# A router between the halves of a projection: logits, ranks and tables of a mixture-of-experts kernel in another order

## The reference

```
x = x + mixer(h) ... @ w_o                       # [1024,1024] @ [1024,1024]
h = rmsnorm(x, norm2_w)
g_prob = softmax(h @ rg_w + rg_b)                # 8 groups
g_sel = the best group, p_group its probability
e_logits = (h @ re_w + re_b)[of the group g_sel] # 8 experts of that group
top_p, top_i = top_k(softmax(e_logits), 2)
gate = p_group * top_p / sum(top_p)
expert = g_sel * 8 + top_i                       # 2 of 64 experts for each token
# every pair (token, expert) is put in its expert's list; then for each expert
hb = silu(xb @ w_gate[e]) * (xb @ w_up[e]);  y[tokens] += gate * (hb @ w_down[e])
x = rmsnorm(x + y, final_norm_w)
```

## Time and profile before

| | |
|---|---|
| median of 3 runs | 2660.02 us (2655.1 to 2666.81) |
| profiled execution | 2654.39 us |
| its span, first to last instruction | 2652.6 us |
| TensorE busy | 2371.0 us, 89% |
| VectorE / ScalarE / GpSimd busy | 765.9 / 551.8 / 574.0 us |
| moved by DMA | 537.41 MB, mean 203 GB/s |
| mean granted TensorE clock | 0.940 |

### The profile page before, as it was taken

How to read it: one execution, slowest core, us unless ns; L and a number is a source line. 1 busy time by engine, 2 the same in 40 slices (tenths; PEclk the granted TensorE clock), 3 DMA queues, 4 the chain that set the end, 5 groups by cost and what they waited for, 6 DMA issues and landing times.

```text
span 2652.6 us, 42516 instructions
## 1 busy us (share of the span) xinstructions
PE 2371.0 (89%) x18656; PEld 1537.5 (58%) x18656; DVE 765.9 (29%) x1615; ACT 551.8 (21%) x1147; POOL 574.0 (22%) x409
## 2 busy tenths in 40 slices
PE   7999988788699999999999997999999988888882
PEld 6887776677576654788887455433334434444440
DVE  4111325555345524223223352211111111111114
ACT  4111223332455412211111221101001111011012
POOL 5333433332111113423322001111111111111110
PEclk9999999998799999999999997999999899999996
DMA  4223110101110022211113306999999999999997
GB/s 188 87 98 126 70 65 27 35 11 73 65 64 1 1 88 72 80 47 49 50 55 126 145 24 263 428 429 430 429 429 429 429 430 428 427 427 429 427 412 209
DMA packets 69777, 537.41 MB, mean 203 GB/s; under 512 B 13464, under 2 KB 13720, under 8 KB 43600
## 3 DMA queue, kind: packets, MB, share of 16 engines
q1 hardware_dynamic: 54688, 501.79, 46.0%
q10 hardware_dynamic: 4656, 15.99, 2.0%
q0 software_dynamic: 10240, 16.82, 1.7%
HBM read 503.08 MB, written 43.52 MB: 206 GB/s over the span
## 4 chain that ended last, share of the span: by engine, by line
PE 71%; DMA 17%; DVE 5%; ACT 4%; issue 3%; ACTq 0%; POOL 0%; POOLq 0%; DVEq 0%; SPq 0%
PE banks L219 47%; DMA arena<-in_wg 15%; PE banks L224 8%; PE banks L226 8%; PE banks L225 7%; DMA arena<-yb 1%; ACT arena L229 1%; ACT arena L1594 1%; PE banks L2800 1%; DVE arena L1573 0%; DVE arena L2776 0%; DVE arena L1121 0%; DVE arena L1141 0%; DMA arena<-in_x 0%; DVE arena L828 0%
## 5 line engine op out<-in xcount | busy, mean ns | idle before, releaser
L219 PE MATMUL banks<-arena 64*64 64x64 f32 (+14 forms) x15424 | 1697.8, 350 | 200.8 <-DMA arena<-in_wg 62.2
L219 PEld LDWEIGHTS banks<-arena 64*64 64x64 f32 (+5 forms) x15424 | 980.0, 157 | 859.9 <-issue 706.0
L229 ACT ACTIVATE arena<-banks 128x512 f32<-128x512 f32 (+6 forms) x381 | 219.8, 587 | 1434.3 <-PE banks L219 624.2
L2794 POOL DMA_INDIRECT yb<-arena x64 | 64.7, 1012 | 810.2 <-DVE arena L2905 810.2
L2905 DVE TENSOR_SCALAR arena<-banks,arena 128x512 f32<-128x512 f32 x64 | 48.1, 751 | 524.3 <-PE banks L219 524.3
L224 PE MATMUL banks<-h1h,w2s 128*128 128x512 f32 x448 | 176.8, 395 | 1.7 <-DVE h1l L1959 1.7
L225 PE MATMUL banks<-h1l,w2s 128*128 128x512 f32 x448 | 174.9, 390 | 0.0
L226 PE MATMUL banks<-h1h,w2s 128*128 128x512 f32 x448 | 174.7, 390 | 0.0
L224 PE MATMUL banks<-hh,wlo 128*128 128x512 f32 x432 | 172.5, 399 | 0.0
L226 PE MATMUL banks<-hh,wlo 128*128 128x512 f32 x432 | 171.1, 396 | 0.0
L225 PE MATMUL banks<-hl,wlo 128*128 128x512 f32 x432 | 169.8, 393 | 0.0
(11 more groups left out here) (240 smaller groups left out, 1522.8 us busy)
## 6 DMA issues: line engine op xcount, KB each, us to landing
arena<-in_wg SPq DMA_DIRECT2D x64, 2048.0 KB, 31.5
arena<-in_wu SPq DMA_DIRECT2D x64, 2048.0 KB, 24.5
arena<-in_wd SPq DMA_DIRECT2D x64, 2048.0 KB, 32.7
arena<-in_w SPq DMA_DIRECT2D x55, 512.0 KB, 3.2
spill<-arena SPq DMA_DIRECT2D x27, 512.0 KB, 2.6
arena<-spill SPq DMA_DIRECT2D x27, 512.0 KB, 5.9
arena<-in_wo SPq DMA_DIRECT2D x16, 512.0 KB, 7.3
arena<-in_x SPq DMA_DIRECT2D x12, 512.0 KB, 5.3
```

The lines of the kernel that those rows point to most:

```text
L219: return pe.e.matmul(o, l, r, start=start, stop=stop)
L229: return act.e.activation(o, i, ACT.Copy)
L2794: return pool.e.indirect_dma_start(yb, bass.IndirectOffsetOnAxis(ap=six[:, col:col + 1].bitcast(U32), axis=0), src[:, :], None, bounds_che ...
```

## The change

TensorE now does the logits of block j-1 between the two projection halves of block j, then the second half, then `pe_count(j - 1)` and `pe_table(j - 2)`. At the end come logits 7, table 6, count 7 and table 7. In `pe_count` the matmuls over older blocks come ahead of the wait for `expert_hot`, then the triangular one that completes the ranks, and the running total last. VectorE runs the route of block j-1 between its two residual adds of block j, norms block j, and makes the table of block j-1 behind that. GpSimd zeroes the three `xg` buffers in `pool_table`, ahead of the last two one-hot rows, instead of one by one ahead of the gathers.

```diff
--- before.py
+++ after.py
@@ -2482,14 +2482,16 @@
                     pe.wait_ge(s(f"wo{c}"), 32)
                     t = mm(pe, u.t[:, :], yT[:, c, j * 128:(j + 1) * 128], wo2[:, c, n * 512:(n + 1) * 512], c == 0, c == 7)
                 t.then_inc(u.full.sem, 1)
+
+                if n == 0 and j:
+                    pe_logits(pe, j - 1)
             if j:
-                pe_logits(pe, j - 1)
-            if j >= 3:
-                pe_table(pe, j - 3)
+                pe_count(pe, j - 1)
+            if j >= 2:
+                pe_table(pe, j - 2)
         pe_logits(pe, 7)
-        pe_table(pe, 5)
+        pe_table(pe, 6)
         pe_count(pe, 7)
-        pe_table(pe, 6)
         pe_table(pe, 7)
         for key in ("count", "tables"):
             ps.release(key)
@@ -2510,21 +2512,19 @@
         for c in range(8):
             t = mm(pe, u.t[:, 0:72], h2T[j % 2][:, c, :], rw[:, c, :], c == 0, c == 7)
         t.then_inc(u.full.sem, 1)
-        if j:
-            pe_count(pe, j - 1)
 
     def pe_count(pe, j):
 
         uc = ps["count"]
         pe.wait_ge(s("con2"), 16)
+        u = ps.open(pe, ("rank", j))
+        for i in range(j):
+            mm(pe, u.t[:, 0:64], C("ones"), Ah[:, i, :], i == 0, False)
         pe.wait_ge(s("expert_hot"), j + 1)
+        mm(pe, u.t[:, 0:64], K2("tri"), Ah[:, j, :], j == 0, True).then_inc(u.full.sem, 1)
         tc = mm(pe, uc.t[:, 0:64], C("ones"), Ah[:, j, :], j == 0, j == 7)
         if j == 7:
             tc.then_inc(uc.full.sem, 1)
-        u = ps.open(pe, ("rank", j))
-        for i in range(j):
-            mm(pe, u.t[:, 0:64], C("ones"), Ah[:, i, :], i == 0, False)
-        mm(pe, u.t[:, 0:64], K2("tri"), Ah[:, j, :], j == 0, True).then_inc(u.full.sem, 1)
 
 
 
@@ -2540,11 +2540,21 @@
     def pool_table(pool):
         pool.wait_ge(s("con2"), 16)
         for n in range(16):
+            if n == 14:
+                pool_zero_xg(pool)
             pool.wait_ge(s("rank_found"), n // 2 + 1)
             if n >= 4:
                 pool.wait_ge(s("table_step"), n - 3)
             pool.e.tensor_scalar(ohm[n % 4][:, :], K2("im"), rk_[:, n % 2, n // 2:n // 2 + 1], None,
                                  ALU.is_equal).then_inc(s("rows").sem, 1)
+
+    def pool_zero_xg(pool):
+
+        pool.wait_ge(s("h2"), 8)
+        u = ps["logits", 7]
+        pool.wait_ge(u.full, u.v)
+        for i in range(3):
+            pool.e.memset(xg[i][:, :], 0.0).then_inc(s("xg_zero").sem, 1)
 
     def dve_table(dve, j):
         e = dve.e
@@ -2620,10 +2630,8 @@
                 u = ps["out2", j, n]
                 dve.wait_ge(u.full, u.v)
                 dve.e.tensor_tensor(xres[:, j, ns], xres[:, j, ns], u.t[:, :], ALU.add).then_inc(u.free.sem, 1)
-            if j:
-                dve_route(dve, j - 1)
-            if j >= 2:
-                dve_table(dve, j - 2)
+                if n == 0 and j:
+                    dve_route(dve, j - 1)
             dve.wait_ge(s("res2_sq"), j + 1)
             dve.e.tensor_scalar(m, m, 1.0 / D, 1e-6, ALU.mult, ALU.add).then_inc(s("res2_mean").sem, 1)
             dve.wait_ge(s("res2_root"), j + 1)
@@ -2636,8 +2644,9 @@
 
             dve.e.scalar_tensor_tensor(h2[j % 3].rearrange("p (c n) -> p n c", c=8), xres[:, j, :].rearrange("p (n c) -> p n c", c=8),
                                        m, n2b.rearrange("p (n c) -> p n c", c=8), ALU.mult, ALU.mult).then_inc(s("h2").sem, 1)
+            if j:
+                dve_table(dve, j - 1)
         dve_route(dve, 7)
-        dve_table(dve, 6)
         dve_table(dve, 7)
         dve_table_out(dve)
 
@@ -2943,7 +2952,6 @@
         for j in range(5, 8):
             pool.wait_ge(*h2_stored(j))
         for i in range(3):
-            pool.e.memset(xg[i][:, :], 0.0).then_inc(s("xg_zero").sem, 1)
             pool.wait_ge(s("xg_zero"), i + 1)
             pool_fetch(pool, i)
         for e in range(NEXP):
```

## The result

| | before | changed |
|---|---|---|
| median of 20 runs each | 2658.14 us | 2667.11 us |
| ratio, 95% interval | | 1.0029 (1.0022 to 1.0037) |
| profiled execution, and its span | 2654.39, 2652.6 | 2666.17, 2664.4 us |
| router's start | 1457.56 | 1460.81 us |
| start to A (last projection half full) | 141.15 | 157.84 us |

The changed kernel is slower by 0.29%, 9.0 us by the medians and 7.7 us by the ratio. That lies inside the whole range (2658 to 2677 us) and inside that of the forecast case alone (+3 to +13 us). The changed kernel's router began 3.25 us later in its profiled execution.

The account below looks back on a forecast made before the run. The experts' weight stream was taken to set the pace, so the end moves with G: A 16.8 us later, A to G 6.9 us shorter, sum +9.9 us, 2664.3 us profiled, 2669.9 us carried to the median; range 2658 to 2677 us.

Parts of the forecast that it names:

- forecast case: Whole kernel: the main case, +9.9 us with its own range of +3 to +13; chance 0.60.
- What bounds the kernel: Expert stage: the weight stream at 429 GB/s sets the pace, so the end moves as G moves.
- G: The moment when the gate projection of expert 0 is full; before, 42.2 us after A.
- The stall in block 1: Router, block 1: TensorE waits at logits 0 for h2 of block 0, 6.4 us.
- Its clock: Behind the block 1 stall: TensorE's granted clock falls to 0.50, costing 4.3 us (bounds 0 and 6.0).
- A itself: Last projection half full: 16.8 us later, from 6.1 us of work moved ahead of it and 10.7 of stall and clock.
- A to G: Router tail to first gate projection: 35.3 us in place of 42.2, 6.9 us better (5.5 to 10.2).
- The gather under the stream: First gather, now lying under weight chunks 3 to 7: 6.5 us, where it took 3.22 before.
- The store of h2 7: Tail, block 7: issued at A + 5.85, lands at A + 18.7, 3 us before it is needed.
- wait in every block: Rival, middle blocks: h2 comes later than TensorE reaches the logits; +16 us at 1 us a block; chance 0.15.
- The clock did fall: Against the rival that the clock does not fall behind the block 1 stall, +5 us; chance 0.12.
- the stream did run dry: Against the rival that the weight stream never runs dry and the end follows A alone, +4 us; chance 0.10.

Follow-up runs that it names:

- Late gain waits: Changed kernel with VectorE's waits for norm gain, router bias and constants moved to their first use; ratio to before 1.0009 (0.9999 to 1.0019).
- busy stall: Changed kernel with 7 added projection matmuls in block 1 ahead of the wait for h2; ratio to before 1.0019 (1.0009 to 1.0030).
- chunk 7 behind gather: Changed kernel with weight chunk 7 issued only when the first gather has landed; ratio to before 1.0007 (0.9996 to 1.0018).
- early adds, short lead: Changed kernel with VectorE's three waits at first use, count 5 and table 4 behind the last projection half; ratio to before 0.9992 (0.9980 to 1.0005).
- second comparison: The changed kernel itself, unaltered, timed once more beside the kernel before; ratio 1.0025 (1.0012 to 1.0038).
- order alone: Kernel before with only the changed order in pe_count and the memsets ahead of the last one-hot rows; ratio to before 0.9993 (0.9980 to 1.0005).
- all together: Changed kernel with late waits, count 5 and table 4 behind the last half, chunk 7 behind the first gather; ratio to before 0.9973 (0.9963 to 0.9984).

## Why the prediction held, step by step

*What bounds the kernel.* Shown: start to G moved by 193.80 - 183.33 = +10.5 us, the last scatter moved with it, and G to the last scatter is 963 us (1.7 more in two) in the slower kernels and in those that gain. The stream is dry ahead of G and full behind 1700 us, as predicted.

*The stall in block 1.* Predicted 6.4 us, measured 6.77. Late gain waits shows it by taking most of it away. *Its clock*: predicted 4.3 us; start to A grew by 16.69, less 6.06 and 6.77 leaves 3.9. Late gain waits gives the same from rows: transposes and the 52 instructions behind took 1.97 + 19.31 us in the changed kernel and 1.09 + 16.20 there, 4.0 us less. That the clock falls because of the length of the idle time is what the prediction assumed, and it is not shown: it fell behind 1.38 us as well (busy stall).

*A itself.* 16.8 predicted, 16.7 measured. That it is so near is in part luck: the stall was 0.4 us longer and the clock cost 0.4 us less than in the sum.

*A to G.* 6.9 us better predicted, 6.2 measured. Three terms in it were off and cancelled for the most part, which is luck too. The clock stayed up through the transposes of block 7 (1.09 us, not 1.97), h2 ended 0.2 us sooner than in the sum, and TensorE's work from logits 7 to rank 7 took 4.7 us, not 5.1; so rank 7 was read at A + 16.0 and not 17.5, and the gather started at A + 20.35, not 21.9. The gather under the stream was mis-sized: 6.5 us predicted between bounds of 3.2 and 7.9, measured 8.2 and 8.4, above the upper bound. From its landing to G it took 7.4 us, not 6.9. That the stream slows the gather was right (chunk 7 behind gather). The idle time behind A, 3.1 us in the prediction, is 2.95 by its own terms; it was 3.29, since TensorE's work there took 2.4 us and not 2.9.

*The store of h2 7* was rightly seen as the next thing to be late, and rightly as not yet late: it landed at A + 17.1 (18.7 predicted), 3.3 us ahead of the gather's start.

*The rivals.* No wait in every block appeared (0.78 us, as before). The clock did fall behind the stall, and the stream did run dry between chunk 7 and G (share 0.12). The gather did not wait for the whole stream (early adds, short lead).

*The size in the end.* +9.9 predicted, +10.5 to G, +9.0 by medians, +7.7 (5.8 to 9.8) by the ratio. The time from the last scatter to the end of the span varies between 46.8 and 49.4 us in these ten profiled executions, with no order that I can see, and was 1.8 us shorter in the changed one. What keeps the timed difference 1 to 3 us under the shift of G stays open; it is no more than that spread, but the second comparison (1.0025, 6.7 us) lies under it too.

## What to carry to other kernels

When a consumer is moved ahead of work that used to stand in front of it, look at its first turn in the loop and not at the steady state: here blocks 1 to 6 had cover, and block 0, behind the stage's own loads, paid 10.6 us, clock included. Find the moment that the end hangs on, here the first gate projection, and what is queued in front of it: the 6.1 us of work moved ahead of the last projection half delayed that half by their full length, and the shorter tail (6.2 us) only just paid for that. And a small transfer that now starts early may start under a big one; holding back one chunk that nobody yet waits for was worth 3.6 us.

## What the runs showed of the hardware

The first gather took 3.2 to 3.7 us while the last of a single weight chunk moved (before, order alone: the DMA share was 0.99 and 0.95 in the first microseconds and fell to 0.19 and 0.47 at its end). It took 4.3 to 4.5 us with only the rest of four weight chunks in flight, and 7.9 to 9.0 with a fifth chunk behind them.

Nearly the same idle time ahead of the transposes was followed by either clock. With 1.38 us (busy stall) the granted clock then fell to about half, with 1.47 us (late gain waits) it stayed at 1.00; with 1.72 us (all together) it fell, with 1.73 us (early adds, short lead) it did not. In the tail before, it stayed at 0.50 over 18.2 us of transposes, logits, ranks and tables, of which TensorE was busy 17.2.
